# A chunked recurrent scan: rolled loop with staged operands, against a written-out and interleaved order

## What is computed

```python
def step(s, inp):
    r_t, w_t, k_t, v_t, a_t, b_t = inp
    sa = jnp.einsum('bhij,bhj->bhi', s, a_t)
    s = s * w_t[:, :, None, :] + sa[..., None] * b_t[:, :, None, :] + v_t[..., None] * k_t[:, :, None, :]
    return s, jnp.einsum('bhij,bhj->bhi', s, r_t)
```

## Time and profile before

| what | us |
|---|---|
| median of 3 runs | 3597.94 (3590.09 to 3602.43) |
| the profiled execution, its own time | 3596.29 |
| its span in the trace | 3594.7 |
| PE busy over the span | 3263.0 |
| the scan's first and last TensorE record | 1203.85 to 1558.4 |

### The profile page before, as it was taken

One profiled execution on the slowest core, in us unless ns is written; L12 is line 12 of the kernel. 1 busy time (PEld: TensorE's weight loads), 2 busy tenths in 40 slices (PEclk: granted clock), 3 DMA queues, 4 the chain that ended last, 5 costly groups with the idle time before them and its releaser, 6 DMA issues. The chain is left out here.

```text
span 3594.7 us, 63286 instructions
## 1 busy us (share of the span) xinstructions
PE 3263.0 (91%) x25508; PEld 3022.9 (84%) x25508; DVE 1639.7 (46%) x2809; ACT 930.2 (26%) x1681; POOL 298.8 (8%) x399
## 2 busy tenths in 40 slices
PE   7999999988999778756888788999998999999997
PEld 7999999987999777734867546888888899999997
DVE  4544544546536233345654253222334544544545
ACT  4222212123104111112455334111124322122212
POOL 0000000012002122200000300000003100000003
PEclk8999999998999898976999899999999899999998
DMA  5111111014322100010100673111122211111102
GB/s 180 35 58 47 35 58 47 23 60 130 101 76 63 59 3 3 3 33 19 45 4 1 181 248 125 44 44 44 38 79 82 67 55 47 35 58 47 35 24 95
DMA packets 255633, 218.47 MB, mean 61 GB/s; under 512 B 39858, under 2 KB 233179, under 8 KB 254812
## 3 DMA queue, kind: packets, MB, share of 16 engines
q1 hardware_dynamic: 250588, 196.34, 17.5%
q0 software_dynamic: 3824, 19.47, 1.5%
q10 hardware_dynamic: 1040, 0.00, 0.0%
HBM read 179.81 MB, written 35.96 MB: 60 GB/s over the span
## 5 line engine op out<-in xcount | busy, mean ns | idle before, releaser
L1222 PE MATMUL banks<-XR,wR 128*128 128x344 f32 x6336 | 1004.4, 320 | 12.6 <-DVE XR L1455 7.8
L1222 PEld LDWEIGHTS banks<-XR,wR 128*128 128x128 f32 x6336 | 1000.3, 189 | 13.4 <-issue 10.0
L1222 PE MATMUL banks<-hidR,wR 128*128 128x344 f32 x3168 | 515.4, 323 | 6.5 <-DVE A L1354 6.5
L1222 PEld LDWEIGHTS banks<-hidR,wR 128*128 128x128 f32 x3168 | 505.1, 190 | 11.7 <-DVE A L1354 11.7
L850 PE MATMUL banks<-XR,gateR 128*128 128x344 f32 x2304 | 398.2, 330 | 14.7 <-DVE gateR L2537 7.9
L850 PEld LDWEIGHTS banks<-XR,gateR 128*128 128x128 f32 x2304 | 371.3, 190 | 30.1 <-issue 8.3
L1354 DVE TENSOR_TENSOR A<-A,banks 128x344 f32<-128x344 f32 x528 | 264.4, 511 | 192.4 <-PE banks L1222 191.5
L1307 ACT ACTIVATE sq<-sq 128x344 f32<-128x344 f32 x132 | 65.1, 493 | 1006.0 <-DVE sq L1334 1006.0
L850 PE MATMUL banks<-XR,pR 128*128 128x344 f32 (+1 forms) x1944 | 317.8, 325 | 8.0 <-DVE XR L1455 4.4
L850 PEld LDWEIGHTS banks<-XR,pR 128*128 128x128 f32 (+1 forms) x1944 | 311.8, 191 | 15.0 <-issue 10.8
L1334 DVE TENSOR_TENSOR sq<-banks,shared 128x344 f32<-128x344 f32 x132 | 68.2, 517 | 418.1 <-PE banks L1222 418.1
(11 more groups left out here) (430 smaller groups left out, 3685.6 us busy)
## 6 DMA issues: line engine op xcount, KB each, us to landing
wraw<-in_ffn_down SPq DMA_DIRECT2D x22, 1024.0 KB, 4.9
wraw<-in_ffn_gate SPq DMA_DIRECT2D x43, 512.0 KB, 3.7
wraw<-in_ffn_up SPq DMA_DIRECT2D x43, 512.0 KB, 4.8
praw<-in_w_in SPq DMA_DIRECT2D x26, 512.0 KB, 4.3
C<-in_cache_mla SPq DMA_DIRECT2D x64, 144.0 KB, 2.4
C<-in_cache_mla POOLq DMA_DIRECT2D x64, 144.0 KB, 2.8
B<-h_spill SPq DMA_DIRECT2D x6, 1376.0 KB, 10.7
h_spill<-A SPq DMA_DIRECT2D x6, 1376.0 KB, 6.3
```

The lines of the kernel that those rows point to most:

```text
L1222: ins = self.k.nc.tensor.matmul(out, wgt[:, a, cols], x(b)[:, grp(g)], start=first and n == 0, stop=last and n == 2)
```

## The change

The stage `rwkv_scan` is written anew. What each matmul, mask, copy and sum computes is the same, and so is their number. Different are:

1. The loop is gone: the 16 chunks are written out in Python, in nine passes p = 0..8 over pairs of chunks, and all semaphore waits are on constants. The small semaphore increments by TensorE after its waits (`settled`) are gone.
2. POOL's copies of the operands and of the decay are gone. Matmuls read `A` and `C` where they lie; the two halves of the moving operand of a gram, which lie in `A` and in `C`, are read through one view `scan_ar` of a single allocation, as two strips of 64 columns. DVE reads `chunk_decay` in place.
3. The carried part of pair p-1 stands between the steps of pair p: W, U, S of its first chunk (a) between grams and turned; W, U, S of its second (b) and both O in the levels, one piece after the Ys of a level (F1 in the text below) and one after its Zs (F2). Pass 0 has no such pieces, pass 8 has nothing else.
4. G1, G2, Vm, Bm, Km and TT have a second buffer for every chunk of a pair, the state a third one; the PSUM banks are given to products, not to chunks.
5. In W, S and O the matmuls that add into one place are no longer issued back to back for one q; q = 0 and q = 1 alternate. Two of the three ACT copies of turned (V and B) are one of twice the width.

```diff
+            for p in range(NP + 1):
+                a, b = 2 * p - 2, 2 * p - 1
+                this, past = p < NP, p > 0
+                if this:
+                    for m in ("g1", "g2", "g3"):
+                        gram(p, 0, m)
+                if past:
+                    carried_in(a)
+                if this:
+                    turned(p, 0, "VB")
+                    turned(p, 0, "K")
+                if past:
+                    solved(a)
+                if this:
+                    gram(p, 1, "g1")
+                    gram(p, 1, "g2")
+                if past:
+                    state(a)
+                if this:
+                    gram(p, 1, "g3")
+                    turned(p, 1, "VB")
+                    turned(p, 1, "K")
                 for l in LV:
+                    if this:
+                        inner(p, 0, l)
+                        inner(p, 1, l)
+                    if past:
                         if l == 2:
+                            carried_in(b)
+                        elif l == 4:
+                            state(b)
                         else:
+                            output(*{8: (a, (2,)), 16: (b, (0,)), 32: (b, (2,))}[l])
+                    if this:
+                        outer(p, 0, l)
+                        outer(p, 1, l)
+                    if past:
+                        if l == 2:
+                            solved(b)
+                        else:
+                            output(*{4: (a, (0, 1)), 8: (a, (3,)), 16: (b, (1,)), 32: (b, (3,))}[l])
```

The products themselves, `inner` being Y and `outer` Z:

```diff
+            def gram(p, s, m):
+                c = 2 * p + s
+                at = slice(c * CH, (c + 1) * CH)
...
+                    left = bt if m == "g1" else kt
+                    ins = both(lambda h, q: mm(k.ps[b][64 * q:64 * q + 64, h * 2 * CH:(h + 1) * 2 * CH]
+                                               .rearrange("p (a t) -> p a t", a=2), lane(left, h, q),
+                                               k.scan_ar[64 * q:64 * q + 64, h:h + 25:24, at]))
...
+            def carried_in(c):
+                z, s = c // 2 % 2, c % 2
+                if c:
+                    dve_s.wait(pe, ("state", c - 1))
...
+                for h in H4:
+                    for q in R2:
+                        mm(lane(out, h, q), lane(kn, h, q), lane(ST[c % 3], h, q), stop=False)
+                    for q in R2:
+                        ins = mm(lane(out, h, q), lane(G2[z][s], h, q), lane(Vm[z][s], h, q), start=False)
...
+            def inner(p, s, l):
+                i = LV.index(l)
+                pool_s.wait(pe, ("level", p, s, l))
+                dve_s.wait(pe, ("T", p, s, LV[i - 1]) if i else ("first", p, s))
+                if i == 0:
+                    dve_s.wait(pe, ("G2", p, 1))
+                pe_s.done(both(lambda h, q: mm(lane(half(Yb[s], 0, CH), h, q), lane(NT_[s], h, q), lane(Tm[s], h, q))),
+                          ("Y", p, s, l))
```

On DVE the order of a pass is the masks of chunk 0, its first terms, G1 and G2 of chunk 1, then sum and decay of the state (a), then chunk 1's first terms:

```diff
+                if this:
+                    masked(0)
+                    first(0)
+                    masked(1)
+                if past:
+                    state(a)
+                if this:
+                    first(1)
```

```diff
+            def state(c):
+                new = ST[(c + 1) % 3]
+                pe_s.wait(dve, ("S", c))
+                dve_s.done(nc.vector.tensor_tensor(new, ST[c % 3], half(Sb, 0, CH), ALU.add), ("sum", c))
+                dve_s.wait(dve, ("sum", c))
+                dve_s.done(nc.vector.tensor_tensor(new, new, k.chunk_decay[:, c, :].unsqueeze(2).to_broadcast([P, RT, RN]),
+                                                   ALU.mult), ("state", c))
+                dve_s.wait(dve, ("state", c))
```

More of the change, by code:

```diff
@@ L324, in rwkv_scan @@
[L324 to L336, removed]
@@ L348, in rwkv_scan @@
[L348 to L354, removed]
@@ new lines, in rwkv_scan, with lane @@
+    Vm, Bm = ([[view(VB[z][s], m * NU, CH) for s in R2] for z in R2] for m in R2)
+    Km = four(room, 24 * NU, CH)
+    TT = four(work, 0, CH)
+    Tm, NT_, Ym, Wm, Um = (two((4 + 2 * m) * NU) for m in range(5))
+    ST = [view(work, 14 * NU, CH), k.ST, k.st_rows]
+    Yb, Zb, Wb, Sb, Ob = (0, 1), (2, 3), 5, 6, 7
+    def half(b, lo, c):
+        return k.ps[b][:, lo:lo + RT * c].rearrange("p (h c) -> p h c", h=RT)
+    def lane(t, h, q, lo=0, c=64):
+        return t[64 * q:64 * q + 64, h, lo:lo + c]
@@ L369, in _ @@
         def _(pool):
[L370 to L384, removed]
-                    for s in R2:
[L386 to L390, removed]
@@ new lines, in turned @@
+            def turned(p, s, m):
+                c = 2 * p + s
+                if s:
+                    act_s.wait(pe, (m, p, 0))
+                elif p:
+                    if m == "VB":
+                        dve_s.wait(pe, ("T", p - 1, 1, LV[-1]))
+                    else:
+                        act_s.wait(pe, (m, p - 1, 1))
+                for n, src in enumerate((now(k.C, 16, c), now(k.A, 4, c)) if m == "VB" else (now(k.C, 12, c),)):
+                    dst = half(3 if m == "VB" else 4, n * NU, CH)
+                    ins = both(lambda h, q: mm(lane(dst, h, q), lane(src, h, q),
+                                               k.ident[64 * q:64 * q + 64, 64 * q:64 * q + 64]))
+                pe_s.done(ins, (m, p, s))
@@ new lines, in solved @@
+            def solved(c):
+                z, s = c // 2 % 2, c % 2
+                act_s.wait(pe, ("W", c))
+                dve_s.wait(pe, ("T", c // 2, s, LV[-1]))
+                pe_s.done(both(lambda h, q: mm(lane(half(Wb, NU, CH), h, q), lane(TT[z][s], h, q), lane(Wm[s], h, q))), ("U", c))
+            def state(c):
+                z, s = c // 2 % 2, c % 2
+                act_s.wait(pe, ("U", c))
+                act_s.wait(pe, ("K", c // 2, s))
+                if c:
+                    dve_s.wait(pe, ("state", c - 1))
+                out = half(Sb, 0, CH)
+                for h in H4:
+                    for q in R2:
+                        mm(lane(out, h, q), lane(Bm[z][s], h, q), lane(Um[s], h, q), stop=False)
+                    for q in R2:
+                        ins = mm(lane(out, h, q), lane(Km[z][s], h, q), lane(Vm[z][s], h, q), start=False)
+                pe_s.done(ins, ("S", c))
```

332 lines of the change are left out of this document (157 added, 175 removed).

## The result

The changed kernel takes 3485.45 us (median of 4 runs, 3478.32 to 3490.02), the kernel before 3595.77 us (median of its 4 runs): a ratio of 0.9691, with a 95% interval of 0.9665 to 0.9716. Forecast were 3488 and a range of 3474 to 3508. The profiled execution of after took 3490.02, with a span of 3488.4.

A forecast was written before the change was run, and what follows sets the result against it. TensorE was taken as the bound, with 27.8 us of work in each 44.3 us iteration. Passes of 26.6 + 207.2 + 13.9 made a 247.7 us stage, ending 110.1 us earlier: 3488 us, range 3474 to 3508.

The forecast's parts named there:

- The reaction of 1.24 us: In the levels, time from TensorE's last issue before DVE's sums to the matmul of chunk 1 that needs them: 1.24 us.
- the waits of the levels: TensorE's waits for DVE's sums at levels 2, 4, 8 and 16: 0.30, 0.07, 0.42, 0.42, together 1.2 us a pass.
- The wait for first terms: TensorE waits 0.6 us a pass for chunk 1's first terms, which DVE computes after the state of (a).
- A pass: One steady pass over a chunk pair: 27.8 + 0.6 + 1.2 = 29.6 us; seven such passes 207.2.
- rivals 3 and 4: 3: instruction stream slower than its bursts, 3522 or halfway 3508, chance 0.06; 4: stalls at every block, 3708, chance 0.03.
- Pass 0: First pass, without carried part: 20.3 us of work plus gaps, first terms and a cold start, 26.6 us.
- pass 8: Last pass, nothing but the chain of the carried part with its copies: 13.9 us including the last copy.
- the start: With POOL's copies gone, TensorE starts the scan at about 1201.1 instead of 1203.85.
- Rival 2: The low clock stays in half of an iteration's 4.5 busy us at 1.2 GHz: 16 us more, 3504; chance 0.06.
- Rival 1: The filler doesn't fill: level gaps stay at 0.77 us, a pass takes 32.0, 17 us more, 3505; chance 0.15.
- my own case: The main forecast, 3488 us, its own range 3475 to 3496; chance 0.66.
- Reading in place at no cost: Grams reading operands as two 64-column strips stay at 54 ns a record; at worst 58.6, 0.3 us a pass.

The follow-up runs named there:

- written-out kernel: The kernel before with only the loop changed: its eight iterations written out, with waits on constants; 3547.95 us, ratio 0.9865.

## Why the prediction was right

- **What bounds the kernel.** Right: 27.8 us of matmul work a pair at 29.3 and 54 ns a record. The whole gain came from TensorE's pauses and its low clock. DVE and ACT are about as busy as before (112.5 us for 117.5, 62.8 for 63.8), POOL has lost its copies (58.4 for 89.7).
- **The reaction of 1.24 us was mis-sized for the new kernel.** It is 1.13 in after (0.35 of F2, 0.47 of Y0 and 0.31 of wait at level 16 of pass 1). The step that failed is "waits on constants instead of register arithmetic: the sequencer does both ahead of the array". The written-out kernel has levels 3.44 apart, 0.14 less, with all else as before. With it the waits of the levels are 0.2, 0, 0.3 and 0.3, not 0.30, 0.07, 0.42 and 0.42.
- **The wait for first terms**, 0.6 in the sum, is 0.3 (0.32 in pass 1, 0.36 in pass 3): the same shorter reactions, and DVE's chain from sum to last first term is 2.3 us (1292.64 to 1294.97) where I had 2.4.
- **A pass** without stalls is 29.0, not 29.6: 4.2 us less in seven.
- **The supply of instructions came in small,** in a form between rivals 3 and 4, to which I had given 0.06 and 0.03: gaps inside runs, as in 3, at the coming of a block, as in 4, but at few of the blocks, and at a quarter or less of the price of 3 (20 to 34 us). The pace between gaps stayed at 29.3 ns a record, so rival 3 as worded did not come. The evidence against the two in the text was that runs of 96 records have no gap, and that a block takes 0.97 us of one DMA engine. Both are so, and neither says how long before its end a block is asked for. Passes 1 to 7 have 4.6 us of such stalls (207.6 - 7 x 29.0). They and the 4.2 above cancel: my 207.2 for the seven passes against 207.6 is luck to that extent. Lucky is the whole time too: the forecast took the rest of the program to stay as it was, the profiled execution was 5.1 longer behind the stage and came to 3490.02 for 3486.2, and the median, 3485.45, is that of four executions that lie 12 us apart.
- **Pass 0** was 26.1 (26.6), **pass 8** with the last copy 13.4 (12.8 to the last record; the sum had 13.9), **the start** 1200.44 (1201.1): together 1.7 us less than the sum had. Of the start, 0.56 is luck: the stage opened that much earlier. TensorE began 0.04 after the opening, where the sum had 0.1. In pass 8 the pause at each copy is 0.69 to 0.70 us, 0.67 beyond the step of a record, where the sum had 0.87, and the clock did not go to the low level.
- **Rival 2, the low clock, did not come**: the passes stand at 1.00. It went with the loop, as the written-out kernel shows.
- **Rival 1 did not come**, but the sign that I gave for it was put one level too early. The 3.9 of my own case and the 4.3 of the rival both hold the 0.42 behind F2 of level 8, which falls between the Y0 of levels 16 and 32. There it is 3.84, where a pass has no stall. Between those of 8 and 16 the sum has 0.07, and it is 3.50 (1303.48 to 1306.98), which is work alone.
- **Reading in place at no cost**: right: the first grams of pass 3, 64x128 by two strips, take the 2.2 us of before, and the stage was 1.8 us shorter for it inside, 1.9 at the start. **Alternation at no cost**: 0.35 us a pass would have come on top without it.
- **The rule of the Trainium skill** that a straight program hides its fetching (Runtime: NRT & Kernel Launch, Instruction fetch mechanics) holds here for most blocks and fails for some: TensorE takes an instruction every 14.6 ns, and seven passes had 4.6 us of stalls. The estimate that I drew from its 20 cycles, 26 us more, did not come either: the pace within runs stayed at 29.3 ns a record. The same section says that a taken branch to a place outside the instructions at hand stalls the fetch, and there the runs agree so far: the 3.56 us pause at each turn of the loop is gone in the written-out kernel.

The gain by part, by the scan's length: 48.9 us for the loop (its pauses, the low clock that they cause, register waits), 1.8 for operands in place and 1.9 more before the first gram, 33.1 for banks, buffers, finer waits and what else changed with them, 24.1 for the interleaving. I had spoken of the third as "the rest"; it is the second largest.

What stays open: what makes a block late. A gap ends 2.2 to 2.9 us after the transfer of the block has begun, and a block is used up in 256 x 14.6 = 3.75 us where nothing waits. If a block is asked for when the one before it begins to be used, an estimate of the slack is thus 0.9 to 1.6 us; no run shows when it is asked for, nor why that was late at some blocks and not at others. Open is also how much of the 33.1 us is worth which of its edits.

## What to carry to other kernels

Count what a hardware loop costs TensorE three times: the pause at the branch, the low clock behind it, and the register arithmetic in every wait on a critical chain. With small matmuls back to back on both halves of the array, the supply of instructions can matter (here 4.6 of 207.6 us); look for waits put to issue in the middle of a group, and shift the code by part of a block (256 instructions) before believing a small difference between two such kernels. Compute a wait as reaction time less what stands in between, put the filler in front of the instruction that waits, not behind it, and look what the filler itself waits for.

## What the runs showed of the hardware

- TensorE stood in straight code, in the middle of groups that wait for nothing, in seven passes for up to 1.15 us at a time (1.65 with the small increments), 1.2 to 1.6 us after an instruction block had landed. Where it did moved with the boundaries of the blocks of 256 instructions: 168 instructions more made a stage 3.0 us shorter.
- 33 small semaphore increments a pass on TensorE made a stage 14.9 us longer, through that supply and the low clock behind one gap, and cost next to nothing through the reaction (28.9 us in a pass that is free of stalls). In a row they cost 0.15 us each.
- A wait whose value is computed in registers made the chain from matmul to vector sums and back 0.14 us longer.
- Matmuls of one quarter of the array issued back to back ran as fast as alternated ones but for 0.35 us a pass, over all the pairs of W, S and O that were reordered.
